# Routed experts: GpSimd loads the down matrices block by block with indirect transfers, SP loads gate and up alone

## The chip, the cores and the metric

One core of one Trainium2 chip runs the whole program. The time is the device time of one execution in microseconds (us). Engines are called PE (TensorE), DVE (VectorE), ACT (ScalarE), POOL (GpSimd) and SP (SyncE, which here only issues transfers).

## The reference

Two transformer blocks follow each other over 512 tokens of width 1024, in float32. The change touches only the last large stage, the routed experts of the second block. Cut to what matters:

```
scores = sigmoid(u @ w_router);  top_e = top 8 of 64 experts (within 4 of 8 groups)
xb  = u_pad[toks]                                   # tokens of one expert, gathered
hid = silu(xb @ we_gate[e]) * (xb @ we_up[e])       # 1024 -> 256
y   = (hid @ we_down[e]) * ws[:, None]              # 256 -> 1024
routed = segment_sum(y, token)                      # added back to the tokens
```

Each expert has three matrices of 1024 KB: gate, up and down.

## The kernel before

**Plan.** The tokens of an expert are cut into half blocks of 64 rows. DVE and PE work out a plan on the chip: the half blocks, sorted by expert, are dealt to four lanes, each lane taking a quarter of the list in order. One block holds 128 rows: block `b` with `p = b % 2` takes the next half block of lanes `2p` and `2p+1`. There are 48 blocks (24 pairs). Where a lane's next half block has the same expert as the one before it, the weights stay where they are; such a stretch is a run, and each run loads its expert once, into the lane's slot of `moe["gu"]` (gate and up) and of `moe["dn"]` (down). So each lane has one slot only, and a new matrix can be loaded once the last product that reads the slot is through.

**SP.** SP goes through the runs in order (`run(m)` reads expert, lane and the block that frees the slot, three register loads; `load` waits and issues). For each run it issues gate, then up, then down:

```
with sp.Fori(4, runs) as m:
    of = run(m)
    load(m, of, "we_gate", "gate_through", KD, ...)
    load(m, of, "we_up", "up_through", KD, ...)
    load_down(m, of)
```

Each `load` waits for two things: that the previous transfer of the same matrix kind has landed, and that the slot is free (`gate_through` is counted by ACT's SiLU, `up_through` and `down_through` by PE's last matmul). SP is one queue, so a wait for the down slot also holds the gate and up of the next run.

**PE.** For block `b`: the up phase (`block_up`, 64 matmuls, gate half then up half), the first four transposes of the next block's rows, two transposes of the hidden rows, the other four transposes, and the down phase (`block_down`, 16 matmuls). Both phases begin with `loads_needed(b)`, a register load of how many loads must have landed.

**ACT and DVE.** ACT copies the transposed rows (`block_rows`) and does the SiLU (`block_gate`). DVE multiplies by the up half (L2920), copies the transposed hidden rows (L2926) and scales the result into `moe["y"]` (L2934).

**POOL.** POOL serves the tokens: `gather` (L841, L844) fetches the 128 rows of a block from DRAM, three blocks ahead, `scatter` (L848, L854) adds the block's result back to DRAM, `weights` (L859) copies a column. Both are indirect transfers of 4 KB rows. A row whose index is out of bounds moves nothing. The order in POOL's queue is gather, scatter, weights, for each block; two scatters are never in flight together (`y_added`).

Of the kernel before, what the change touches and what calls it, by code (L numbers as in the profile page):

```python
# [7 lines left out]
P = 128  # L8
# [3 lines left out]
TT = T // P  # L12
# [13 lines left out]
E = 64  # L26
# [39 lines left out]
MAX_BLOCKS = MAX_HALVES // 2  # L66
PAD_ROW = 4 * T
# [3 lines left out]
def two_blocks(nc, A, out_T, u_rows, y_rows):  # L71
    f32 = mybir.dt.float32
    f32r = mybir.dt.float32r
    ALU = mybir.AluOpType
# [4 lines left out]
    with ctx:  # L79
# [109 lines left out]
        def rounded(name, shape, at):  # L189
# [63 lines left out]
                      for i, at in enumerate((split_at + 4 * (FT - 8) * T, arena_at + 4 * (ple["end"] + 12 * T)))]  # L253
# [21 lines left out]
                       shift=(2,)))  # L275
# [11 lines left out]
                                                      "own_key", "own_halves")] +  # L287
# [32 lines left out]

        rows_in = [ints(f"rows_in{i}", 1, u32) for i in range(2)]
# [281 lines left out]
        for v in range(STEPS):  # L603
# [7 lines left out]
            n = len(maps)  # L611
# [21 lines left out]
        def _(sp):  # L633
# [43 lines left out]
            def load_down(m, of):  # L677
                load(m, of, "we_down", "down_through", 2, moe["dn"])
# [12 lines left out]
            for m in range(2):  # L691
                of = run(m)
                load_up(m, of)
                load_down(m, of)
# [4 lines left out]
            load_down(2, of2)  # L699
            load_down(3, of3)  # L700
            with sp.Fori(4, runs) as m:
# [3 lines left out]
                load_down(m, of)  # L705
# [19 lines left out]
        def _(pool_eng):  # L725
# [114 lines left out]
            def gather(b, p):  # L840
                pool_eng.tensor_copy(rows_in[p][:, :], moe["idx"][:, bass.ds(b, 1)]).then_inc(S("rows_known"), 1)  # L841
                pool_eng.wait_ge(S("rows_known"), b + 1)
# [4 lines left out]
            def scatter(b, p, added):  # L847
# [7 lines left out]
                                            bounds_check=2 * Y_ROWS - 1, oob_is_err=False, compute_op=ALU.add).then_inc(S(f"y_added{p}"), 16)  # L855

# [19 lines left out]
            pool_eng.wait_ge(S("second_zeroed"), 16 * (TT - 2))  # L876
            scatter(0, 0, 1)
# [20 lines left out]
        def _(pe):  # L898
# [747 lines left out]

            def hidden_transposes(b, p):
# [5 lines left out]
            def block_down(b, p):  # L1653
                needed = loads_needed(b)
                for k in range(2):
                    pe.wait_ge(S("hT_done"), b * 2 + (k + 1))
                    if k == 0:
                        pe.wait_ge(S("we_down_in"), needed)
                    for half in range(2):
                        if k == 0:  # L1660
                            pe.wait_ge(S("y_copied"), b * 2 + (2 * TT + half - 1))
# [11 lines left out]
            def block(b, p, gathers):  # L1673
# [3 lines left out]
                hidden_transposes(b, p)  # L1677
                block_transposes(b + 1, 1 - p, gathers, 1)
# [4 lines left out]
            block(0, 0, 1)  # L1683
            with pe.Fori(1, pairs) as i:


                for b, p in ((i * 2 + (-1), 1), (i * 2, 0)):
                    block(b, p, i + 1)
# [1398 lines left out]
```

## Time and profile before

| | |
|---|---|
| median of 3 runs | 2215.12 us (2207.13 to 2215.75) |
| the profiled execution, its own time | 2209.77 us |
| its span in the profile | 2207.8 us |
| PE busy in the span | 97% |
| DVE, POOL, ACT busy | 55%, 34%, 32% |
| routed experts, first to last block | about 1585 to 2183 us |

The span runs from the first to the last instruction and is 2.0 us short of the execution's own time. In the routed experts (from about 1585 us) PE repeats one block after another, and 16 DMA engines carry weights, gathered rows and scattered rows side by side. A transfer issued by SP goes through queue q1, one issued by POOL through queue q0.

### The profile page before, as it was taken

The page shows a single profiled execution, that of the slowest core. Times are in us where ns is not written, and L with a number is a line of the kernel's source. Part 1 is how long each engine was busy: PE and PEld are TensorE (multiplying, and loading weights), DVE is VectorE, ACT ScalarE, POOL GpSimd, SP SyncE. Part 2 cuts the span into 40 slices and gives each one's busy share as a digit, 9 for nine tenths or more (in the row PEclk, how much of TensorE's full clock was granted, in tenths as well). Part 3 has the DMA queues.
Part 4 walks back from the last instruction along what each step waited for, and adds up shares of the span by engine and source line. Part 5 has one row for each costly group of instructions (what it writes and reads, how often), then busy time and mean ns, then how long its engine had stood idle before and what let it go on. Part 6 is the DMA issues. An engine that isn't in the chain of part 4 may idle for free.

```text
span 2207.8 us, 31566 instructions
## 1 busy us (share of the span) xinstructions
PE 2136.7 (97%) x11810; PEld 1536.7 (70%) x11811; DVE 1207.6 (55%) x1891; ACT 716.5 (32%) x1116; POOL 740.6 (34%) x462
## 2 busy tenths in 40 slices
PE   6999999999999999999999999999999999999898
PEld 5877567788878767777777778876565555555555
DVE  5566655889981448599999684246412112122113
ACT  5335664333342334344444345123111111111112
POOL 4331123434444324333333356441122222222222
PEclk9999899999999999999999999999999999999999
DMA  4220122454634212333333213322778899999885
GB/s 165 77 96 1 68 77 78 167 175 158 210 131 151 86 60 85 98 105 102 100 104 102 91 58 115 115 100 86 287 239 310 283 336 321 311 332 352 298 286 186
DMA packets 165535, 358.73 MB, mean 162 GB/s; under 512 B 12016, under 2 KB 101232, under 8 KB 146624
## 3 DMA queue, kind: packets, MB, share of 16 engines
q1 hardware_dynamic: 143360, 304.00, 38.3%
q0 software_dynamic: 15088, 38.69, 7.2%
q10 hardware_dynamic: 6992, 14.75, 2.0%
q8 instruction: 63, 1.03, 0.2%
q14 instruction: 32, 0.26, 0.0%
HBM read 340.87 MB, written 33.10 MB: 169 GB/s over the span
## 4 chain that ended last, share of the span: by engine, by line
PE 86%; DMA 5%; ACT 3%; DVE 2%; POOL 2%; issue 1%; SPq 0%; ACTq 0%; POOLq 0%; DVEq 0%
PE bank L911 25%; PE bank L1643 14%; PE bank L1334 12%; PE bank L1664 7%; PE bank L1233 4%; PE bank L1413 3%; DMA arena<-in_we_gate 2%; PE bank L1622 2%; PE bank L1047 1%; PE bank L1420 1%; DMA arena<-in_w_up 1%; PE bank L1498 1%; PE bank L920 1%; PE bank L921 1%; PE bank L1082 1%
## 5 line engine op out<-in xcount | busy, mean ns | idle before, releaser
L1643 PE MATMUL bank<-arena,hn 128*64 128x256 f32 x3072 | 346.7, 384 | 12.3 <-DMA arena<-in_we_gate 11.5
L1643 PEld LDWEIGHTS bank<-arena,hn 128*64 128x64 f32 x3072 | 232.8, 139 | 138.5 <-issue 43.9
L805 POOL TENSOR_TENSOR w_low_flat<-arena,in_high 128x1024 fp32r<-128x1024 f32 x71 | 184.3, 2617 | 278.4 <-ACT in_high L1968 278.3
L2920 DVE TENSOR_TENSOR inv<-inv,bank 128x128 f32<-128x128 f32 x96 | 23.3, 284 | 327.6 <-PE bank L1643 327.6
L1664 PE MATMUL bank<-arena 128*64 128x512 f32 x768 | 175.4, 598 | 5.1 <-DVE arena L2926 0.5
L772 POOL TENSOR_TENSOR w_low<-arena,w_high 128x2048 fp32r<-128x2048 f32 x22 | 103.7, 4712 | 160.1 <-ACT w_high L1890 160.1
L2934 DVE SCALAR_TENSOR_TENSOR sq<-bank,arena 128x512 f32<-128x512 f32 x96 | 72.1, 751 | 151.3 <-PE bank L1664 149.5
L1334 PE MATMUL bank<-in_x,in_high 128*128 128x512 f32 x384 | 154.2, 402 | 0.0
L1334 PE MATMUL bank<-in_x,w_low_flat 128*128 128x512 f32 x384 | 151.1, 393 | 0.0
L1334 PE MATMUL bank<-x_low,in_high 128*128 128x512 f32 x384 | 150.7, 392 | 0.0
L911 PE MATMUL bank<-x_high,w_high 128*128 128x512 f32 x336 | 133.4, 397 | 1.8 <-POOL w_low L772 1.8
L911 PE MATMUL bank<-x_high,w_low 128*128 128x512 f32 x336 | 132.4, 394 | 0.0
L911 PE MATMUL bank<-x_low,w_high 128*128 128x512 f32 x336 | 132.3, 394 | 0.0
L854 POOL DMA_INDIRECT y_halves<-sq,rows_out x47 | 75.5, 1606 | 155.0 <-DVE sq L2934 151.9
L2255 ACT ACTIVATE inv<-bank 128x256 f32<-128x256 f32 x48 | 18.4, 383 | 333.4 <-PE bank L1643 333.4
L1664 PEld LDWEIGHTS bank<-arena 128*64 128x64 f32 x768 | 52.6, 136 | 97.0 <-issue 96.7
L2250 ACT ACTIVATE hn<-bank 128x512 f32<-128x512 f32 x96 | 57.3, 597 | 185.8 <-PE bank L1622 185.8
L2479 DVE SCALAR_TENSOR_TENSOR arena<-arena,small 128x512 f32<-128x512 f32 x84 | 101.5, 1209 | 3.0
L841 POOL CAST rows_in<-arena 128x1 uint32 (+1 forms) x48 | 8.8, 183 | 262.0 <-PE bank L1622 249.2
L2367 DVE RECIPROCAL inv<-inv 128x512 f32<-128x512 f32 x20 | 67.0, 3352 | 53.9 <-ACT inv L1717 53.9
L744 POOL TENSOR_TENSOR w_low<-arena,z_w_high 128x2048 fp32r<-128x2048 f32 (+2 forms) x12 | 61.9, 5155 | 89.6 <-ACT z_w_high L1727 89.6
L1334 PEld LDWEIGHTS bank<-in_x,w_low_flat 128*128 128x128 f32 x384 | 72.1, 188 | 17.0
(499 smaller groups left out, 4887.2 us busy)
## 6 DMA issues: line engine op xcount, KB each, us to landing
arena<-in_we_gate SPq DMA_DIRECT2D x49, 1024.0 KB, 8.5
arena<-in_we_up SPq DMA_DIRECT2D x49, 1024.0 KB, 9.0
arena<-in_we_down SPq DMA_DIRECT2D x49, 1024.0 KB, 8.4
arena<-in_w_in SPq DMA_DIRECT2D x38, 1024.0 KB, 5.3
arena<-in_w_ada SPq DMA_DIRECT2D x12, 2048.0 KB, 7.8
arena<-in_w_up SPq DMA_DIRECT2D x22, 1024.0 KB, 10.6
arena<-in_w_in SPq DMA_DIRECT2D x17, 512.0 KB, 5.1
arena<-in_w_out SPq DMA_DIRECT2D x4, 2048.0 KB, 9.9
```

Of the source, the lines that this page charges most:

```text
L772: pool_eng.tensor_tensor(up_low(pair), w, up_high(pair).bitcast(f32), ALU.subtract)\
L805: pool_eng.tensor_tensor(in2_tile(j, "low"), in2_tile(j, "whole"), in2_tile(j, "high").bitcast(f32), ALU.subtract).then_inc(S("w_low"), 1)
L854: pool_eng.indirect_dma_start(y_rows, bass.IndirectOffsetOnAxis(rows_out[p][:, :], 0), moe["y"][:, p, :], None, bounds_check=2 * Y_ROWS - ...
L911: ins = nc.tensor.matmul(out, w, x, start=k == 0 and n == 0, stop=k == KD - 1 and n == 2)
L1233: ins = nc.tensor.matmul(banks[DOWN_BANK[t]][:, :], w, x, start=k == HID_ORDER[0] and n == 0, stop=k == HID_ORDER[-1] and n == 2)
L1334: ins = nc.tensor.matmul(banks[i % 2][:, :], w[:, k, :], x, start=k == 0 and n == 0, stop=k == KD - 1 and n == 2)
L1413: nc.tensor.matmul(banks[t][:, :], w[:, P * t:P * t + P], yn_high_tile(k), start=k == 0 and w is high, stop=False)
L1643: ins = nc.tensor.matmul(rows_of(banks[2 + part][:, 0:FE], c), columns_of(moe["xT"][:, p, :], k, c), moe["gu"][:, 2 * p + c, at:at + FE], ...
L1664: ins = nc.tensor.matmul(rows_of(banks[5 + half], c), columns_of(moe["hidT"][:, p, :], k, c), moe["dn"][:, 2 * p + c, at:at + 512], start= ...
L2367: nc.vector.reciprocal(inv[:, j % 2, :], inv[:, j % 2, :]).then_inc(S("qk_inv"), 1)
L2479: ins = nc.vector.scalar_tensor_tensor(out, w[:, k, :], C_ACT[:, k:k + 1], out, ALU.mult, ALU.add)
L2934: nc.vector.scalar_tensor_tensor(moe["y"][:, p, 512 * half:512 * half + 512], banks[5 + half][:, :], moe["wcol"][:, p:p + 1], moe["g2"][:, ...
```

## The change

SP issues gate and up only, except for the first down matrix of each of the four lanes (`first_down`). The other down matrices are loaded by POOL, once for each block: `load_down(b, p, known)` waits until block `b - 2` is through its down phase, copies two columns of row numbers, and issues two indirect transfers, one for each lane of the block. DVE works out the row numbers: in the first half block of a run, row `128 * expert + partition` of the down matrices seen as rows of 8 KB; in all others a number out of bounds, so that the transfer moves nothing. PE no longer reads how many down loads it needs; it waits for 32 per block on `down_loaded0` or `down_loaded1`, and does so (`down_free`) ahead of the second four transposes. PE's loop is shorter by one pair of blocks, which are written out.

```diff
-            def load_down(m, of):
-                load(m, of, "we_down", "down_through", 2, moe["dn"])
+            def first_down(m, of):
+                e, lane, free = of
+                if m > 0:
+                    sp.wait_ge(S("we_down_in"), m * 16)
+                sp.wait_ge(S("down_through"), free)
+                sp.nop(nofuse=True)
+                sp.dma_start(moe["dn"][:, m, :], A["we_down"][bass.ds(e, 1)].rearrange("a (p k) n -> p (a k n)", k=2))\
+                  .then_inc(S("we_down_in"), 16)
...
             with sp.Fori(4, runs) as m:
                 of = run(m)
                 load(m, of, "we_gate", "gate_through", KD, moe["gu"][:, :, 0:KD * FE])
                 load(m, of, "we_up", "up_through", KD, moe["gu"][:, :, KD * FE:2 * KD * FE])
-                load_down(m, of)
...
+            def load_down(b, p, known):
+                pool_eng.wait_ge(S("down_through"), b + 1)
+                pool_eng.tensor_copy(dn_now[p][:, :], dn_rows[:, bass.ds(b * 2, 2)]).then_inc(S("rows_known"), 1)
+                pool_eng.wait_ge(S("rows_known"), known)
+                for c in range(2):
+                    pool_eng.nop(nofuse=True)
+                    pool_eng.indirect_dma_start(moe["dn"][:, 2 * p + c, :], None, A["we_down"].rearrange("e (p k) n -> (e p) (k n)", k=2),
+                                                bass.IndirectOffsetOnAxis(dn_now[p][:, c:c + 1], 0), bounds_check=E * P - 1,
+                                                oob_is_err=False).then_inc(S(f"down_loaded{p}"), 16)
...
             with pool_eng.Fori(2, pairs) as i:
                 pool_eng.wait_ge(S("moe_tr"), i * 4 + (-2))
-                gather(i * 2, 0)
+                gather(i * 2, 0, i * 4 + (-2))
+                load_down(i * 2 + (-1), 1, i * 4 + (-1))
                 scatter(i * 2 + (-3), 1, i)
                 weights(i * 2 + (-1), 1)
                 pool_eng.wait_ge(S("moe_tr"), i * 4)
-                gather(i * 2 + 1, 1)
+                gather(i * 2 + 1, 1, i * 4)
+                load_down(i * 2, 0, i * 4 + 1)
                 scatter(i * 2 + (-2), 0, i)
                 weights(i * 2, 0)
+            load_down(pairs_but_one * 2 + 1, 1, pairs_but_one * 4 + 2)
...
+                if tt == 0:
+                    nc.tensor.matmul(banks[3][:, 2 * P:3 * P], pcol("dn_row").to_broadcast([P, P]), ident, start=True, stop=True)
...
+            def down_free(b, loaded, value):
+                pe.wait_ge(S(loaded), value)
+                for half in range(2):
+                    pe.wait_ge(S("y_copied"), b * 2 + (2 * TT + half - 1))
...
             def block_down(b, p):
-                needed = loads_needed(b)
                 for k in range(2):
                     pe.wait_ge(S("hT_done"), b * 2 + (k + 1))
-                    if k == 0:
-                        pe.wait_ge(S("we_down_in"), needed)
...
                 block_transposes(b + 1, 1 - p, gathers, 0)
                 hidden_transposes(b, p)
+                down_free(b, loaded, value)
                 block_transposes(b + 1, 1 - p, gathers, 1)
                 block_down(b, p)
...
+            step(nc.vector.tensor_scalar(pcol("dn_row"), pcol("new"), -float(NO_ROW), float(NO_ROW), ALU.mult, ALU.add))
+            counted_step(nc.vector.scalar_tensor_tensor(pcol("dn_row"), pcol("expert"), float(P), pcol("dn_row"), ALU.mult, ALU.add))
...
+            nc.vector.tensor_scalar(dn_rows, banks[3][:, 2 * P:3 * P], const("row"), None, ALU.add)
             nc.vector.tensor_copy(moe["ws"], banks[3][:, MAX_BLOCKS:2 * MAX_BLOCKS]).then_inc(S("blocks_known"), 1)
```

PE, in the loop over pairs, from the hidden transposes of a block to its down phase. Before:

```order
L1650 MATMUL bank<-shp,inv 128x128 [waits moe_hid] x2
L1622 MATMUL bank<-shp,hn 128x128 x4
L1632 TENSOR_LOAD shp
L1632 ISA x2
L1661 REGISTER_ALU [waits we_down_in,hT_done]
L1664 MATMUL bank<-arena 64x512 [waits y_copied]
```

The register load (L1632) stands between the transposes and the down phase. The same place in the changed kernel (there L1679 is the hidden transposes, L1646 the row transposes, L1688 the down phase):

```order
L1679 MATMUL bank<-shp,inv 128x128 [waits moe_hid] x2
L1674 REGISTER_ALU [waits down_loaded1]
L1674 REGISTER_ALU [waits y_copied]
L1646 MATMUL bank<-shp,hn 128x128 [waits y_copied]
L1646 MATMUL bank<-shp,hn 128x128 x3
L1688 MATMUL bank<-arena 64x512 [waits hT_done]
```

The register load is gone from between the transposes and the down phase, and the waits for the weights and for the result's banks now stand ahead of the second four transposes.

POOL, in its loop, one half of a turn. Before (L841 and L844 are the gather, L848 and L854 the scatter, L859 the weights):

```order
L841 COPY rows_in<-arena 128x1
L842 REGISTER_ALU
L844 DMA hn<-u_rows,rows_in 128x1024 [waits rows_known]
L848 ISA
L848 COPY rows_out<-arena 128x1
L849 REGISTER_ALU
L850 ISA [waits rows_back]
L852 REGISTER_ALU [waits y_copied]
L854 DMA y_halves<-sq,rows_out 1024x1024 [waits y_added0]
```

Between the gather and the scatter stand a copy and its wait only. The same place in the changed kernel (L852 is the gather, L867 to L871 the down loads, L862 the scatter):

```order
L852 DMA hn<-u_rows,rows_in 128x1024 [waits rows_known]
L867 ISA [waits down_through]
L867 COPY arena<-arena 128x2
L868 REGISTER_ALU
L871 DMA arena<-in_we_down,arena 128x2048 [waits rows_known]
L871 DMA arena<-in_we_down,arena 128x2048
L856 ISA
L856 COPY rows_out<-arena 128x1
L857 REGISTER_ALU
L858 ISA [waits rows_back]
L860 REGISTER_ALU [waits y_copied]
L862 DMA y_halves<-sq,rows_out 1024x1024 [waits y_added0]
```

A copy and two indirect transfers, behind a wait for PE's down phase, now stand between the gather and the scatter.

## Rows read from the trace of the kernel before

**Rows 1.** The page, its first line.

```profile
span 2207.8 us, 31566 instructions
```

**Rows 2.** The stretches view of the expert stage: busy us of each engine, clock, DMA.

```profile
1590.00:2160.00 570.00, 553.88 (x4124) 321.40 (x4122) 113.62 (x276) 72.56 (x138) 146.26 (x226) 0.99 0.87 301
```

**Rows 3.** Waits of PE, 1580 to 2150 us: total us, times, longest.

```profile
PE bank L1643 <- DMA arena<-in_we_gate: 11.5, 2, 6.5
```

**Rows 4.** The chain that ended last, around its two stops: start, us, what.

```profile
1765.03 3.67 PE bank L1664 x16
...
1771.84 7.47 DMA arena<-in_we_gate
...
1788.39 9.41 DMA arena<-in_we_gate
1797.93 8.71 PE bank L1643 x64
...
1808.15 3.65 PE bank L1664 x16
...
2061.81 3.67 PE bank L1664 x16
...
2096.13 9.78 PE bank L1643 x64
...
2107.46 3.65 PE bank L1664 x16
```

**Rows 5.** The timeline of one undisturbed block: start, us, engine, line, operation.

```profile
1619.17 0.60 PE L1622 MATMUL bank<-shp,hn 128*128 128x128 f32 x4
1619.18 0.49 DVE L2926 COPY arena<-bank 128x128 f32<-128x128 f32 x2 [0.23 <-PE bank L1650]
1619.86 3.65 PE L1664 MATMUL bank<-arena 128*64 128x512 f32 x16
...
1620.94 1.07 POOL L844 DMA_INDIRECT hn<-u_rows,rows_in  x1 [0.81 <-POOL rows_in L841]
...
1623.34 7.08 PE L1643 MATMUL bank<-arena,hn 128*64 128x256 f32 x64
...
1625.18 1.60 POOL L854 DMA_INDIRECT y_halves<-sq,rows_out  x1 [2.97 <-DVE sq L2934]
...
1632.03 0.18 POOL L841 CAST rows_in<-arena 128x1 uint32 x1 [5.05 <-PE bank L1622]
```

**Rows 6.** The timeline at the first stop.

```profile
1760.73 0.35 SPq L670 DMA_DIRECT2D arena<-in_we_gate  x1
...
1763.73 0.34 SPq L670 DMA_DIRECT2D arena<-in_we_up  x1
...
1768.91 0.34 SPq L670 DMA_DIRECT2D arena<-in_we_down  x1
...
1772.17 0.38 ACT L2255 ACTIVATE inv<-bank 128x256 f32<-128x256 f32 x1 [6.60 <-PE bank L1643]
...
1789.20 3.65 PE L1664 MATMUL bank<-arena 128*64 128x512 f32 x16
```

**Rows 7.** Waits of SP, 1580 to 2200 us.

```profile
SPq L669 <- PE bank L1664: 96.9, 21, 4.7
```

**Rows 8.** DMA queues, 1765 to 1800 us: packets, MB, share of 16 engines.

```profile
q1 hardware_dynamic: 1605, 11.70, 84.7%
q0 software_dynamic: 738, 1.58, 15.3%
```

**Rows 9.** The timeline ahead of the stage: the last tables of the plan.

```profile
1561.57 3.73 PE L1577 MATMUL bank<-arena 128*128 128x128 f32 x32
...
1563.55 1.22 DVE L2897 TENSOR_TENSOR arena<-arena,shp 128x1024 f32<-128x1024 f32 x1 [3.10 <-PE bank L1577]
...
1574.49 0.28 DVE L2908 TENSOR_SCALAR arena<-bank,shp 128x64 f32<-128x64 f32 x1
```

**Rows 10.** The page, DMA issues of the down matrices: count, KB each, us to landing.

```profile
arena<-in_we_down SPq DMA_DIRECT2D x49, 1024.0 KB, 8.4
```

More of the change, by code:

```diff
@@ L66 @@
 MAX_BLOCKS = MAX_HALVES // 2
+NO_ROW = 1 << 20
 PAD_ROW = 4 * T
@@ L274, in two_blocks @@
                        hidT=(2, 2 * P), wcol=(2,), idx=(MAX_BLOCKS,), ws=(MAX_BLOCKS,), out=(MAX_BLOCKS,),
-                       shift=(2,)))
+                       shift=(2,), dnr=(P,), dnn=(2, 2)))
         moe["X"] = hn[:, 0:4, :].rearrange("p (a b) n -> p a (b n)", a=2)
@@ L319, in two_blocks @@
         block_i = ints("block_i", TT * TOP, i32)
+        dn_rows = moe["dnr"].bitcast(u32)
+        dn_now = [moe["dnn"][:, i, :].bitcast(u32) for i in range(2)]
         rows_in = [ints(f"rows_in{i}", 1, u32) for i in range(2)]
@@ L693, in _ @@
                 load_up(m, of)
-                load_down(m, of)
+                first_down(m, of)
             of2, of3 = run(2), run(3)
@@ L698, in _ @@
             load_up(3, of3)
-            load_down(2, of2)
-            load_down(3, of3)
+            first_down(2, of2)
+            first_down(3, of3)
             with sp.Fori(4, runs) as m:
@@ L704, in _ @@
                 load(m, of, "we_up", "up_through", KD, moe["gu"][:, :, KD * FE:2 * KD * FE])
-                load_down(m, of)
             for p in range(2):
@@ L838, in _, with gather @@
                                        ALU.mult).then_inc(S("sh_hid"), 1)
-            def gather(b, p):
+            def gather(b, p, known=None):
                 pool_eng.tensor_copy(rows_in[p][:, :], moe["idx"][:, bass.ds(b, 1)]).then_inc(S("rows_known"), 1)
-                pool_eng.wait_ge(S("rows_known"), b + 1)
+                pool_eng.wait_ge(S("rows_known"), b + 1 if known is None else known)
                 pool_eng.nop(nofuse=True)
@@ L876, in _ @@
             pool_eng.wait_ge(S("second_zeroed"), 16 * (TT - 2))
+            load_down(2, 0, 5)
             scatter(0, 0, 1)
@@ L1672, in _, with block @@
             pairs = pairs_but_one + 1
-            def block(b, p, gathers):
+            def block(b, p, gathers, loaded, value):
                 block_up(b, p)
@@ L1682, in _ @@
                 block_transposes(0, 0, 1, half)
[L1683 to L1688, printed above, removed]
+            block(0, 0, 1, "we_down_in", 32)
+            block(1, 1, 2, "we_down_in", 64)
+            with pe.Fori(1, pairs_but_one) as i:
+                for p in range(2):
+                    block(i * 2 + p, p, i + (p + 1), f"down_loaded{p}", i * 32)
+            block(pairs_but_one * 2, 0, pairs, "down_loaded0", pairs_but_one * 32)
             block_up(pairs_but_one * 2 + 1, 1)
             hidden_transposes(pairs_but_one * 2 + 1, 1)
+            down_free(pairs_but_one * 2 + 1, "down_loaded1", pairs_but_one * 32)
             block_down(pairs_but_one * 2 + 1, 1)
```

5 lines of the change are left out of this document (2 added, 3 removed).

## The prediction

> **What bounds the kernel now.** The page's first line gives the span to set the sum against [rows 1]. The stretches view of the expert stage shows who is full: PE is busy 553.9 of 570 us at a granted clock of 0.99, while the DMA engines are busy 0.87 of the time [rows 2]. So the stage is bound by PE, with the DMA engines close behind. The list of waits says how little PE waits: 11.5 us in two pieces, both for a gate matrix [rows 3]. The chain that ended last gives the full price of the two stops. From the down phase at 1808.15 to the one at 2061.81 lie 21 blocks, so one block takes 253.66 / 21 = 12.08 us. From 1765.03 to 1808.15 there are three blocks, which should take 36.2 us and take 43.1: 6.9 us lost. From 2061.81 to 2107.46 again three blocks, 45.6 us: 9.4 us lost. That is 16.3 us, more than the wait of 11.5, because the up phase behind each stop takes 8.7 and 9.8 us where an undisturbed one takes 7.1 [rows 4, 5]. What the change can win on transfers is at most these 16.3 us. Anything else must come out of the 12.08 us of a block.
>
> **Part 1: SP no longer waits for the down slot.** SP waited 96.9 us in 21 pieces for PE's down phase [rows 7]; the question is which of these waits reaches PE. At the first stop it does. The gate and up of a lane go out at 1760.73 and 1763.73. Then SP stands until the down phase ends at 1768.7, issues down at 1768.91, and 2.93 us later (register loads) the gate of the next lane [rows 4, 6]. From there the chain is three landings of gate matrices one behind the other, the last of 9.4 us, and PE goes on at 1797.93, when it wanted to at 1789.20 + 3.65 = 1792.85 [rows 4, 6].
>
> In the changed kernel SP issues the second gate 2.93 us after the up at 1763.73, at about 1766.7, 5.2 us sooner. If that one lands within 6 us, the third gate goes out when its slot is free, behind the SiLU that ends at 1772.55 [rows 6], at about 1772.8, and the fourth when the third has landed. PE wants the fourth at 1792.85, so two landings have 20.0 us: the stop is gone if a landing takes 10.0 us or less.
>
> How long is a landing then? In the burst q1 moves 11.70 MB in 0.847 of 35 us, which is 2.66 us of all engines for one matrix of 1.05 MB, and q0 takes 5.4 us for the gathers and scatters of three blocks, 1.8 us a block [rows 8]. Three matrices in flight behind each other today make 3 x 2.66 / 0.847 = 9.4 us, which is what the chain shows (7.5 and 9.4) [rows 4]. After the change q1 holds only two matrices, 5.3 us if q0 is idle. But q0 then carries two down matrices a block on top, 2 x 2.66 + 1.8 = 7.1 us of work. If two busy queues share evenly, that takes 14.2 us, more than a block, so in a burst q0 always has work, and a landing takes 2 x 2 x 2.66 = 10.6 us. Two of them miss the 20.0 us by 1.2. Between the ends 5.3 and 10.6 I stand near the upper one, since both queues are full there. I leave 2.5 us at each stop for what remains, the slower clock behind a stop included, and book **11 us** of the 16.3. The bounds are 16.3 (both stops gone) and nothing. The bytes don't change: a matrix is loaded once for each run, as before, and a row out of bounds costs next to none of the engines' time, as with the padding rows of the gathers that are in the 1.8 us.
>
> **A rule that speaks against it.** The row above shows q1 taking 84.7% while q0 has little to do, and says nothing of two full queues. The Trainium skill, "DMA: Bandwidth & Descriptors", section "SWDGE vs HWDGE vs iDMA", states that the software and hardware paths feed different queues inside each DMA engine, between which the engine takes turns. By that rule the landing is the 10.6 us end, and of the 11 us the stops give back still all but 1.2 us each before the clock's share. The same page, section "Rules for kernel authors", says that spreading transfers over issuing engines gives no bandwidth and only saves issue time; that would put all of the gain into the 5.2 us of SP's earlier issue. It makes of the two stops 10.4 us instead of 11.
>
> **Part 2: PE between the transposes and the down phase.** In an undisturbed block the second four transposes start at 1619.17 and end at 1619.77, and the down phase starts at 1619.86 [rows 5]. A following group can begin before its forerunner's end: the up phase starts at 1623.34, 0.17 us before the down phase's end at 1623.51. So the down phase could start at 1619.60. Its operand isn't what is late: DVE's first copy of two ends at 1619.43 [rows 5]. The 0.26 us belong to what PE's queue holds there: a register load, its two followers and the waits for weights and banks, all behind the transposes. The register load goes, and the waits move ahead of the second transposes, where they may cost some of it again. So the gain is between 0 and 0.26 us; in 47 blocks 0 to 12. I take 0.15, as three waits with register arithmetic remain: **7 us**. The waits themselves are long satisfied outside bursts (the banks since DVE's scaling of the block before). In a burst a late down matrix would now also hold four transposes, 0.6 us, which ACT needs before the next up phase; it has 3.65 us of down phase as cover.
>
> **Part 3: POOL.** New in each block are a copy, a wait for it, and two indirect transfers. The wait is 0.81 us, a gather costs 1.07 and a scatter 1.60 [rows 5]. The trace has no indirect transfer of 8 KB rows. The nearest is the gather, same direction and as many rows, so 0.2 + 0.8 + 2 x 1.07 = 3.1 us; with the dearer 1.60, 4.2 us; if the price goes by bytes on top of that, 3.2 us each and 7.4. POOL is idle for 5.05 us ahead of the next gather, and the new work can start some 0.9 us before today's scatter could, since it waits for PE's end and not for DVE's scaling [rows 5]. So there are 6.0 us of room, and at 3.1 or 4.2 the cost is **0**. Queued behind the new work is the scatter, 2 to 3 us later; the result buffer it must empty is wanted two blocks on, and at 12.08 us a block that is covered. The gather behind it is three blocks ahead of use. The down matrix itself is issued about 2 us after the down phase of block b - 2 and wanted some 20 us later: with the 14.2 us above it is in time.
>
> **Part 4: the start.** DVE has an added operation of 128 columns ahead of the copy on which the first gather waits; the like one of 64 columns takes 0.28 us [rows 9]. PE has one more matmul in front of 32 that take 3.73 us, 0.12 us each [rows 9]. Together **0.5 us** more. DVE's two one-column operations lie before the tables, where DVE waits 3.10 us for PE later on [rows 9]. Without that cover they would cost about as much as that operation, 0.3 us each.
>
> **The sum:** 2207.8 - 11 - 7 + 0.5 = 2190.3 us of span, 2192.3 with the 2.0 outside it. The profiled execution (2209.8) stands 5.3 us under the median of the runs (2215.1), which themselves lie 8.6 apart. 17.5 us off the one is 2192.3 and off the other 2197.6; I write 2197.
>
> **Rivals.**
> - **Only one of the two gains comes.** The stops are merely moved, since the DMA engines are at full share either way, or the wait ahead of the transposes costs what the register load did. For it: DMA is busy 0.87 on average [rows 2]. Against it: the first stop's chain begins with SP's wait. It leaves 5 to 10 us, 2205 to 2210: not to be told from no change, since about 0.5% (11 us) is what a measurement of this kernel can tell.
> - **The evenly shared queues make new stops.** The down matrices of q0 are wanted 8 us later than the gates of the same block, yet get half of the engines. Wherever three or four lanes change together, a gate lands after 10.6 us or more (12.4 if a block's whole q0 work goes first), 2 x 12.4 - 20 = 4.8 us at each of the two stops and perhaps as much at four more stretches: 29 us lost instead of 16.3, less the 7 of part 2: 2221. It decides from a landing of 11.5 us. By the skill's rule of taking turns, named above, the stop would be 1.2 us and this rival would not come.
> - **POOL becomes the bound.** If an indirect transfer of 8 KB rows costs POOL 3.2 us, each block needs 7.4 - 6.0 = 1.4 us more than it has, 64 us in 46 blocks, less the 24 us that the gathers are ahead: 40 slower, 2248 with part 2. It decides from 2.5 us each. Against it: the gather's 1.07.
> - **The change doesn't do what it says**, and the out-of-bounds rows are moved or are dear: 96 down matrices instead of 49 [rows 10] would be 47 x 2.66 = 125 us of DMA in a stage that has 74 free: some 50 us slower. The gathers' padding speaks against it.
>
> **How the numbers follow.** Forecast 0.52, one gain only 0.28, new stops 0.10, POOL 0.07, rows not skipped 0.03. The likeliest's own range is 2184 to 2206. The range 2183 to 2224 takes in the second and third case and leaves out POOL, the skipped rows and some of both sides. Faster by over 0.5%: 0.52; within: 0.29; slower: 0.19.
>
> **What would show it.** Right: no SP wait for the down phase; at both places where today the chain shows gate matrices, PE waits under 3 us; the down phase 0.1 to 0.25 us nearer to the transposes; two POOL transfers of 1.1 to 1.6 us before each scatter; a block of about 11.9 us. Wrong: waits of PE for gate or down matrices elsewhere, a gather that PE waits for, POOL transfers of over 2.5 us, or a block of 12.1 us.

## The result

The changed kernel took 2200.23 us (median of 6 runs, 2195.37 to 2204.64), the kernel before 2214.38 us on the same chip (6 runs, 2205.67 to 2216.81). The ratio is 0.9948, with a 95% interval of 0.993 to 0.9966: faster by about 11.5 us, by just over 0.5%. The ratio takes in all runs; the two medians alone lie 14.2 us apart. Run again in a later session it gave 0.9949 (0.9931 to 0.9968). The prediction was 2197 us.

The page of the changed kernel, its first line, comes first, then the stretches view of the expert stage (us; busy us of PE, weight load, DVE, ACT, POOL; granted clock; share of the DMA engines; GB/s).

```profile
span 2202.8 us, 31560 instructions
```

```profile
1590.00:2160.00 570.00, 564.49 (x4192) 319.47 (x4190) 113.81 (x276) 73.00 (x139) 248.27 (x367) 0.99 0.87 304
```

Against [rows 1, 2]: the span is 5.0 us shorter, less than the 11.5, since the profiled execution of the changed kernel was its slowest (2204.64 us) and that of the kernel before lay under its median (2209.77 against 2214.38). PE is busy 10.6 us more of the same 570 us, at the same clock, and the DMA engines are as busy as before. POOL has 102 us more to do, and none of PE's waits below is for POOL's own work.

The waits of PE (us in total, times, longest), 1585 to 2155 us, then those of SP, 1580 to 2200 us:

```profile
PE bank L1667 <- DMA arena<-in_we_gate: 5.5, 2, 2.9
PE bank L1646 <- DMA hn<-u_rows,rows_in: 3.9, 1, 3.9
```

```profile
SPq L672 <- DMA arena<-in_we_up: 67.9, 16, 5.4
SPq L672 <- PE bank L1667: 61.6, 25, 2.5
SPq L672 <- DMA arena<-in_we_gate: 58.6, 31, 4.8
```

PE waits for a gate in the same two places, 5.5 us where it was 11.5 [rows 3], and nowhere in the blocks for a down matrix. The 3.9 us for gathered rows lie ahead of the first block, at the first gather of all (PE goes on at 1586.26); the kernel before waits there too, 2.65 us, until 1582.41. SP's wait for the down phase (96.9 us [rows 7]) is gone from the loop. SP now waits most for its own transfers.

**Where the time went.** The stage, from the first down phase to the 48th, can be read from two timeline rows of each kernel (start, us, engine, line, operation). Before:

```profile
1595.69 1.90 PE L1664 MATMUL bank<-arena 128*64 128x512 f32 x7
...
2179.88 3.65 PE L1664 MATMUL bank<-arena 128*64 128x512 f32 x16 [0.51 <-DVE arena L2926]
```

After:

```profile
1599.47 1.94 PE L1688 MATMUL bank<-arena 128*64 128x512 f32 x8
...
2174.16 3.65 PE L1688 MATMUL bank<-arena 128*64 128x512 f32 x16 [0.28 <-DVE arena L2957]
```

That is 584.19 us before and 574.69 after, 9.5 less. I split it with the 48 starts: the mean of the periods that hold no stop is the block, and what the 47 periods hold above 47 blocks is what the stops cost. A period counts as holding a stop from 0.3 us above the median of all periods on; where many periods are a little long (down_late, extra_two, no_skip) the split is rough. The same sum for every kernel, from one profile each:

| kernel | stage | block | stops in all |
|---|---|---|---|
| before | 584.2 | 12.08 | 16.2 |
| changed | 574.7 | 12.03 | 9.2 |
| changed, second run | 573.7 | 12.03 | 8.1 |
| one_load | 577.6 | 11.91 | 17.8 |
| waits_ahead | 583.4 | 11.98 | 20.3 |
| waits_behind | 569.9 | 11.92 | 9.8 |
| waits_behind_2 | 569.7 | 11.92 | 9.6 |
| short_loads | 570.8 | 11.91 | 10.8 |
| down_late | 589.6 | 12.08 | 22.0 |
| extra_two | 587.5 | 12.20 | 14.2 |
| sp_still_waits | 592.2 | 12.03 | 27.0 |
| no_skip | 630.5 | 12.08 | 63.0 |

So of the 9.5 us, 7.0 come from the stops (16.2 - 9.2) and 2.4 from the block (0.052 x 47). The second run of the changed kernel differs by 1.1 us in its stops, which says how far a stop total of one profile can be trusted. Ahead of the stage the profiled execution was 3.8 us late, behind it 0.7, which leaves the 5.0 of the span. Most of the 3.8 isn't the change's. DVE's first operation of the plan, ahead of every operation that the change adds, already starts 2.37 us later. Before, it and the first gather's issue, and the same two after:

```profile
1513.41 0.14 DVE L2747 TENSOR_SCALAR arena<-shp 128x1 f32<-128x1 f32 x1
...
1577.16 1.10 POOL L844 DMA_INDIRECT hn<-u_rows,rows_in  x1 [0.93 <-POOL rows_in L841]
```

```profile
1515.78 0.14 DVE L2775 TENSOR_SCALAR arena<-shp 128x1 f32<-128x1 f32 x1
...
1580.00 1.11 POOL L852 DMA_INDIRECT hn<-u_rows,rows_in  x1 [0.93 <-POOL rows_in L849]
```

From the one to the other lie 63.75 us before and 64.22 after: the change costs 0.47 us there. The other 0.94 us lie between the first gather's issue and the first down phase (18.53 us before, 19.47 after). Of these, 0.54 is the first up phase, 9.45 us before and 9.99 after, at mean granted clocks of 0.75 and 0.70. In the second run of the changed kernel the same up phase took 7.13 us at a granted clock of 1.00, so this isn't the change's either. In waits_behind, whose program up to the stage is the same, the first down phase starts at 1594.93, earlier than before. The offset goes with the execution.

**The first stop.** SP's timeline in the changed kernel has the first gate's issue:

```profile
1763.61 0.34 SPq L673 DMA_DIRECT2D arena<-in_we_gate  x1
```

and the chain that ended last goes on from the up (start, us, what):

```profile
1766.62 0.34 SPq L673
...
1767.35 1.23 SPq L661
...
1770.53 8.64 DMA arena<-in_we_gate
...
1779.42 9.62 DMA arena<-in_we_gate
...
1789.29 9.08 DMA arena<-in_we_gate
...
1798.51 8.81 PE bank L1667 x64
```

The second gate goes out 3.9 us after the up of its forerunner, with no wait between, so the cause of [rows 4, 6] is gone. But it is still a chain of three landings, not two: the first takes 8.64 us, so that the third gate, too, waits for a landing and not for its slot, and the fourth's issue is set by landings alone. The stops cost 9.2 us though PE waits only 5.5. The rest is the up phase behind each: at this stop PE stood 2.87 us, then the granted clock was 0.54 from 1798.5 to 1801.5, nearly the lower of its two levels (1.2 of 2.4 GHz), and the up phase took 8.81 us where the one at 1759.49 took 6.93. The queues in the burst, 1765 to 1800 us (packets, MB, share of the 16 engines):

```profile
q1 hardware_dynamic: 1064, 7.80, 54.0%
q0 software_dynamic: 1136, 5.59, 46.7%
```

q0 has gone from 15.3% to 46.7%, q1 from 84.7% to 54.0% [rows 8]: two busy queues share nearly evenly here. The Trainium skill, "DMA: Bandwidth & Descriptors", section "SWDGE vs HWDGE vs iDMA", says that each DMA engine takes turns between the software and the hardware queue. The trace agrees with that; the page gives no shares.

**One block.** The timeline of an undisturbed one:

```profile
1621.87 0.66 PE L1646 MATMUL bank<-shp,hn 128*128 128x128 f32 x4
1622.06 0.48 DVE L2951 TENSOR_TENSOR inv<-inv,bank 128x128 f32<-128x128 f32 x2 [6.22 <-PE bank L1667]
...
1622.40 0.53 PE L1679 MATMUL bank<-shp,inv 128*128 128x128 f32 x2
...
1622.88 0.65 PE L1646 MATMUL bank<-shp,hn 128*128 128x128 f32 x4
1623.46 3.65 PE L1688 MATMUL bank<-arena 128*64 128x512 f32 x16
...
1623.70 0.18 POOL L849 CAST rows_in<-arena 128x1 uint32 x1 [2.01 <-PE bank L1646]
1624.71 1.05 POOL L852 DMA_INDIRECT hn<-u_rows,rows_in  x1 [0.83 <-POOL rows_in L849]
...
1627.31 0.19 POOL L867 COPY arena<-arena 128x2 uint32 x1 [1.54 <-PE bank L1688]
1628.38 1.03 POOL L871 DMA_INDIRECT arena<-in_we_down,arena  x1 [0.88 <-POOL arena L867]
1629.71 1.00 POOL L871 DMA_INDIRECT arena<-in_we_down,arena  x1 [0.30 <-issue]
```

The down phase starts 0.58 us after the second transposes, where it was 0.69 [rows 5]. An indirect transfer that brings 8 KB rows costs POOL 1.0 us, no more than a gather of 4 KB rows. The new work runs from 1627.31 to 1630.71, 3.4 us. POOL keeps 2.0 us of idle time before the next gather, where it had 5.05, and 1.5 before the copy: 3.5 us of room are left.

### The profile page after: what moved, and what is told of

Read it like the earlier page. It is cut to its first block, busy times and chain, and to the rows that moved or that the text cites. A ratio compares the mean times of both kernels' runs of the same rounds, so it can differ in the third digit from the quotient of the medians.

```text
span 2202.8 us, 31560 instructions
## 1 busy us (share of the span) xinstructions
PE 2139.4 (97%) x11812; PEld 1526.5 (69%) x11813; DVE 1214.1 (55%) x1894; ACT 716.2 (33%) x1116; POOL 839.5 (38%) x600
## 3 DMA queue, kind: packets, MB, share of 16 engines
q8 instruction: 64, 1.05, 0.2%
## 4 chain that ended last, share of the span: by engine, by line
PE 85%; DMA 5%; DVE 3%; ACT 2%; POOL 2%; issue 1%; SPq 1%; ACTq 0%; POOLq 0%; DVEq 0%
PE bank L933 25%; PE bank L1667 14%; PE bank L1356 12%; PE bank L1688 7%; PE bank L1255 4%; PE bank L1435 3%; DMA arena<-in_we_gate 2%; PE bank L1646 2%; PE bank L1069 1%; PE bank L1442 1%; DMA arena<-in_w_up 1%; PE bank L1520 1%; PE bank L942 1%; PE bank L1104 1%; PE bank L950 1%
## 5 line engine op out<-in xcount | busy, mean ns | idle before, releaser
L1667 PEld LDWEIGHTS bank<-arena,hn 128*64 128x64 f32 x3072 | 225.5, 139 | 139.0 <-issue 35.4
L1688 PE MATMUL bank<-arena 128*64 128x512 f32 x768 | 175.4, 598 | 0.3 <-DVE arena L2957 0.3
L862 POOL DMA_INDIRECT y_halves<-sq,rows_out x47 | 76.2, 1620 | 110.4 <-DMA y_halves<-sq,rows_out 64.7
L871 POOL DMA_INDIRECT arena<-in_we_down,arena x92 | 92.9, 1010 | 56.2 <-POOL arena L867 39.7
L1688 PEld LDWEIGHTS bank<-arena 128*64 128x64 f32 x768 | 51.1, 136 | 90.4 <-issue 83.0
```

The costliest lines, as they stand in the source:

```text
L862: pool_eng.indirect_dma_start(y_rows, bass.IndirectOffsetOnAxis(rows_out[p][:, :], 0), moe["y"][:, p, :], None, bounds_check=2 * Y_ROWS - ...
L871: pool_eng.indirect_dma_start(moe["dn"][:, 2 * p + c, :], None, A["we_down"].rearrange("e (p k) n -> (e p) (k n)", k=2), bass.IndirectOffs ...
L1667: ins = nc.tensor.matmul(rows_of(banks[2 + part][:, 0:FE], c), columns_of(moe["xT"][:, p, :], k, c), moe["gu"][:, 2 * p + c, at:at + FE], ...
L1688: ins = nc.tensor.matmul(rows_of(banks[5 + half], c), columns_of(moe["hidT"][:, p, :], k, c), moe["dn"][:, 2 * p + c, at:at + 512], start= ...
```

## The experiments

The theory after the result: the stops shrank because SP no longer stands behind the down phase, and what is left of them comes from landings on evenly shared queues; the block got shorter because PE's second register load went, and lost two thirds of that again (0.115 of 0.17 us) to the waits ahead of the transposes. The rivals: the stops shrank through the other queue or the slots alone, whatever SP does; the block got shorter through the moved waits; POOL, or down matrices that come late, already take something. Ratios are against the kernel before, measured on the same chip in the same session.

### one_load: the kernel before, with one register load in PE

```diff
-            def block_down(b, p):
-                needed = loads_needed(b)
+            def block_down(b, p, needed):
...
-                block_up(b, p)
+                needed = block_up(b, p)
...
-                block_down(b, p)
+                block_down(b, p, needed)
```

> The kernel before, with one edit on PE: the down phase uses the count of loads that the up phase of the same block has read, so the register load between the second transposes and the down phase is gone; SP still loads all three matrices, POOL is untouched. Theory (the register load is late at the down phase): the block falls from 12.08 us to 11.90 (11.83 to 12.00), the two stops stay at 6.9 and 9.4 us, the whole is 5 to 11 us faster. Rival (the waits behind the transposes are what is late, or nothing is): the block stays at 12.05 to 12.08, the whole within 2 us of before.

Measured: 2202.98 us, ratio 0.9957 (0.9938 to 0.9976). The block is 11.91 us, 0.17 less, 8 us over the stage; the stops are 17.8 us in all. So this edit alone, without any change to the transfers, gives in the block more than the whole change did there (2.4 us), and nothing in the stops. A third stop, of 1.6 us, has appeared; one profile doesn't say whether the faster blocks made it.

### waits_behind and waits_behind_2: the changed kernel, waits behind the transposes

```diff
-                down_free(b, loaded, value)
                 block_transposes(b + 1, 1 - p, gathers, 1)
+                down_free(b, loaded, value)
```

> The changed kernel with PE's waits for the down matrices and for the result's banks put back behind the second transposes. Theory (in the changed kernel these waits ahead of the transposes cost back a part of what the register load gave): the block falls from 12.04 us to 11.85 to 11.98, 3 to 8 us less in all than the changed kernel (its median was 2200), stops as in the changed kernel (4.8 and 4.6). Rival (waits cost the same in either place, or more next to the down phase): 12.03 to 12.10 a block, within 2 us of the changed kernel or slower.

> The changed kernel with PE's waits behind the second four transposes, once more, for a tighter interval beside the other. If the shorter block is real, the ratio is 0.993 again, with a block of 11.92 us; if the first run was luck it lies at 0.995, as the changed kernel.

Measured: 2195.51 us, 0.993 (0.991 to 0.9951), and again on another chip 2193.82 us, 0.9938 (0.9916 to 0.996). The block is 11.92 us in both, 0.115 shorter than the change's 12.03, 5.4 us over the stage. The timeline shows where. In this kernel:

```profile
1629.78 0.53 PE L1679 MATMUL bank<-shp,inv 128*128 128x128 f32 x2
1630.14 0.60 PE L1646 MATMUL bank<-shp,hn 128*128 128x128 f32 x4
1630.67 3.65 PE L1688 MATMUL bank<-arena 128*64 128x512 f32 x16
```

From the transposes of the hidden values to the second four transposes are 0.36 us, and from there to the down phase 0.53: 0.89. In the changed kernel's block above they are 0.48 and 0.58: 1.06. In its next block they are 0.38 and 0.58, 0.96:

```profile
1634.48 0.53 PE L1679 MATMUL bank<-shp,inv 128*128 128x128 f32 x2
1634.86 0.65 PE L1646 MATMUL bank<-shp,hn 128*128 128x128 f32 x4
1635.44 1.08 PE L1688 MATMUL bank<-arena 128*64 128x512 f32 x4
```

These two alternate through the loop, as blocks of 12.08 and 11.98 us, and the differences of the sums from 0.89 (0.17 and 0.07) are, within 0.01, those of the blocks from 11.92. PE waits for none of the three semaphores there; the time goes all the same, on both sides of the transposes.

It isn't the place of the waits alone. In the changed kernel blocks 0 and 1 are written out ahead of the loop, and their waits, in the same place, are for constants. Block 1 there:

```profile
1610.49 0.53 PE L1679 MATMUL bank<-shp,inv 128*128 128x128 f32 x2
1610.85 0.60 PE L1646 MATMUL bank<-shp,hn 128*128 128x128 f32 x4
1611.38 3.65 PE L1688 MATMUL bank<-arena 128*64 128x512 f32 x16
```

That is 0.36 and 0.53, as in waits_behind, and the period that ends there is 11.91 us; it is 11.91 or 11.92 in after_again, down_late, sp_still_waits and no_skip too, whose PE program is the same. So a satisfied wait for a constant costs nothing that shows. What costs comes with the blocks in the loop, where the values that are waited for are worked out in registers. That it is this arithmetic is likely, but no run changes it alone.

### waits_ahead: the kernel before, one register load, the waits moved ahead

```diff
 (one_load, and)
+            def down_free(b, needed):
+                pe.wait_ge(S("we_down_in"), needed)
+                for half in range(2):
+                    pe.wait_ge(S("y_copied"), b * 2 + (2 * TT + half - 1))
...
+                down_free(b, needed)
                 block_transposes(b + 1, 1 - p, gathers, 1)
-                block_down(b, p, needed)
+                block_down(b, p)
```

> The kernel before with one register load (as in the experiment that left only the second load out, block 11.91 us), and PE's waits for the down matrix and the two banks moved ahead of the second four transposes, as the change has them; nothing of the change on SP or POOL. If those waits, placed there, cost what the runs with and without them put on them (12.03 - 11.92), the block is 12.03 us, 5.4 us more over the stage than with the register load alone, and the ratio is 0.998. If the 0.115 us comes from something else of the change (its two semaphores, POOL's transfers), the block stays at 11.91 and the ratio at 0.996.

Measured: 2209.23 us, 0.999 (0.9974 to 1.0006). Neither number of the two expectations: the block is 11.98 us. The waits in that place cost 0.07 us here, some 60% of the 0.115. The block is as long as the shorter of the two blocks of the changed kernel, and its block 0, the only one with constants for the banks, again shows 0.36 and 0.53 us. The other 0.05 is the 0.1 us that every second block of the changed kernel takes more, and comes with something else of the change; its waits for down matrices, on one of two semaphores against the loop's counter, are the candidate, but no run takes that apart. The stops are 20.3 us against 17.8 in one_load; one execution of each doesn't say whether the waits did that.

### sp_still_waits: the changed kernel, SP still behind the down phase

```diff
                 load(m, of, "we_up", "up_through", KD, moe["gu"][:, :, KD * FE:2 * KD * FE])
+                sp.wait_ge(S("down_through"), of[2])
+                sp.nop(nofuse=True)
```

> The changed kernel, in which SP after each run's up matrix waits until the down slot is free, as it did before, but issues nothing then. Theory (the smaller stops of the changed kernel come from SP no longer standing in that wait): the stops grow from 4.7 and 4.5 us to 6.5 to 10 each and there may be a third; the block stays at 12.03 us; 4 to 12 us slower than the changed kernel. Rival (the stops are smaller because the down matrices no longer stand in q1's line between the gates, whatever SP waits for): stops of 4 to 5.5 us, within 2 us of the changed kernel.

Measured: 2220.8 us, 1.004 (1.0027 to 1.0053), slower than before. SP's and PE's waits:

```profile
SPq L715 <- PE bank L1690: 112.0, 25, 4.7
```

```profile
PE bank L1669 <- DMA arena<-in_we_gate: 13.5, 7, 6.1
PE bank L1669 <- DMA arena<-in_we_up: 5.6, 6, 1.6
```

The block is that of the changed kernel, the stops are 27.0 us instead of 9.2, nine instead of two. With the down matrices on POOL's queue and SP's wait kept, the gates go out about as late as before and land later, while q0 takes 48.5% of the engines. At the first stop 10.6 us lie between the first gate's issue and the second's (11.1 before, 6.9 in the changed kernel), and the three landings take 9.6, 9.2 and 9.8 us (7.5, 8.6 and 9.4 before). All of the gain in the stops thus comes from SP's earlier issue, and with SP held back the shared queues cost 11 us (27.0 - 16.2). This is the rival of new stops as it looks when SP doesn't get ahead.

### down_late: the changed kernel, POOL's loads behind the scatter

```diff
-                load_down(i * 2 + (-1), 1, i * 4 + (-1))
                 scatter(i * 2 + (-3), 1, i)
                 weights(i * 2 + (-1), 1)
+                load_down(i * 2 + (-1), 1, i * 4 + (-1))
```

> The changed kernel with POOL's order scatter, weights, down loads instead of down loads, scatter, weights; the down matrices reach queue q0 some 3 us later in each block. Theory (in a burst the two queues share the engines evenly, and the down matrices of q0 hold up the gates of q1): the gates land sooner and each stop falls from 4.7 us to 2 to 3.5, 2 to 5 us less in all; the scatter waits less for the one before. Rival A (the stop is set by the bytes of a burst or by SP's own chain): stops of 4.5 to 5. Rival B (the down matrices are now late): PE waits for them, slower than the changed kernel.

Measured: 2211.21 us, 1.0005 (0.9987 to 1.0023): all of the gain is gone. PE's waits:

```profile
PE bank L1646 <- DMA arena<-in_we_down,arena: 13.0, 6, 3.0
```

and the chain, at a stop of 4.3 us:

```profile
1782.90 0.76 DVE sq L2965
...
1784.59 0.09 POOL y_halves L862
...
1787.40 1.05 POOL arena L871
1788.75 19.60 DMA arena<-in_we_down,arena
1808.57 1.11 PE bank L1646 x4
```

No gate stops PE any more. Now the down matrices do: their issue stands behind the scatter, which waits for DVE's scaling, and the landing takes 19.6 us. My estimate of it was 14.2. This is rival B of the expectation. As the change orders them they are in time; some 3 us later they are the bound.

### extra_two: the changed kernel, two more indirect transfers a block

They bring nothing anywhere: all of their rows are out of bounds, and the result is the same.

```diff
                                                 oob_is_err=False).then_inc(S(f"down_loaded{p}"), 16)
+                for c in range(2):
+                    pool_eng.nop(nofuse=True)
+                    pool_eng.indirect_dma_start(nowhere[:, 2 * p + c, :], None, ...,
+                                                bass.IndirectOffsetOnAxis(no_rows[:, c:c + 1], 0), bounds_check=E * P - 1,
+                                                oob_is_err=False).then_inc(S(f"down_loaded{p}"), 16)
...
(the waits for down_loaded: i * 64 instead of i * 32)
```

> The changed kernel with two more indirect transfers on POOL in each block, all of whose rows are out of bounds, so that they move nothing; this adds 2 x 1.3 us to POOL's chain of a block, where the changed kernel leaves it 2.0 us idle. Theory (POOL has slack of its own and is some two blocks ahead): 0.6 us a block too much, 28 us over the stage, eaten by the lead of about 24 us: 0 to 6 us slower than the changed kernel. Rival (POOL's chain reaches PE at once): 0.6 x 46 = 28 us slower or more.

Measured: 2215.82 us, 1.0015 (0.9996 to 1.0033). That is some 16 us slower than the changed kernel, between the 0 to 6 of the theory and the 28 of the rival: neither was right. The groups of POOL from 1590 to 2160 us (line, engine, operation, names, count | busy us, mean ns of one | idle before):

```profile
L874 POOL DMA_INDIRECT arena<-in_we_down,arena x88 | 88.7, 1008 | 52.4 <-POOL arena L870 38.5 <-issue 13.9
L879 POOL DMA_INDIRECT nowhere<-in_we_down,no_rows x88 | 88.3, 1004 | 26.8 <-issue 26.8
```

A transfer that moves nothing costs POOL as much as one that moves 1 MB in 8 KB rows, 1.00 us, and 0.30 between two: 2.6 us more a block, of 3.5 that were left. From the timeline of one block:

```profile
1727.07 1.63 POOL L865 DMA_INDIRECT y_halves<-sq,rows_out  x1 [1.04 <-PE bank L1656]
...
1737.39 0.66 PE L1656 MATMUL bank<-shp,hn 128*128 128x128 f32 x4
1737.87 0.49 DVE L2961 TENSOR_TENSOR inv<-inv,bank 128x128 f32<-128x128 f32 x2 [6.52 <-PE bank L1677]
...
1738.15 1.63 POOL L865 DMA_INDIRECT y_halves<-sq,rows_out  x1 [1.04 <-issue]
```

Behind a long wait for a scatter, POOL works through a block in 11.08 us without a gap, from scatter to scatter, still under PE's 12.0. It isn't the bound even now, it only catches up slowly. What makes the block 12.20 us is DVE: its first product starts 0.48 us after the transposes in this block and 0.3 to 0.4 in most, 0.19 in the changed kernel (1621.87 and 1622.06 above), and PE waits for it. DVE's own rows are no longer than before (284 ns against 283), and what holds it back I didn't trace. So the causal step from POOL's extra work to DVE's delay is not shown. With 8 us of blocks (0.17 x 47), 5.0 of stops and 4.3 ahead of the stage, the span is 17.7 us longer than the changed kernel's. So POOL's own time isn't what costs here, but more work on POOL isn't free either.

### no_skip: the changed kernel, down matrices loaded for every block

```diff
-step(... pcol("dn_row"), pcol("new"), -float(NO_ROW), float(NO_ROW), ...)
+step(... pcol("dn_row"), pcol("new"), 0.0, 0.0, ...)
```

The same matrices are loaded again in each block; the result is the same.

> The changed kernel with the row numbers in bounds in every half block, so that each down matrix is loaded again for every half block (96 loads instead of 49). It prices the skipping. Theory: 47 x 2.66 = 125 us more work for the DMA engines, of which 70 to 75 us were free: 40 to 70 us slower than the changed kernel, with PE waiting for gate and down matrices through the whole stage. Rival (a skipped row costs nearly as much as a moved one): within 10 us of the changed kernel.

Measured: 2259.65 us, 1.0216 (1.0196 to 1.0236), 48.6 us slower than before. The stretches view of the stage:

```profile
1590.00:2190.00 600.00, 559.50 (x4030) 309.41 (x4030) 108.92 (x268) 70.70 (x135) 236.88 (x350) 0.96 0.96 354
```

The DMA engines are at 0.96 now, the granted clock of PE is down to 0.96 as well, and the stops take 63 us. The transfers on POOL, all with rows now, cost it 1013 ns each, against 1010 where half of them are skipped. The rival of rows that aren't skipped was priced at some 50 us. Not skipping costs 59 us against the changed kernel, 48.6 against the kernel before, so the price was about right, and the change isn't it.

### short_loads: waits_behind, SP's register loads without their range checks

```diff
 (waits_behind, and for the expert and the lane, but not for the count of free slots)
-                        sp.value_load(plan[...], min_val=0, max_val=3),
+                        nc.values_load(plan[...], engines=[SP], ..., skip_runtime_bounds_check_because=...)
```

> The changed kernel with PE's waits behind the second transposes (median 2195.5) and with two of SP's three register loads of each run without the run-time check of their range, which takes some 0.6 us off SP's way from an up to the next gate. Theory (SP's register loads stand in the chain of gates that ends in a stop): each stop is 0.3 to 0.8 us shorter, 1 us in all, not to be told from that kernel by time. Rival (the chain is set by the landings alone): stops of 4.8 to 5.0 as there.

Measured: 2194.41 us, 0.9927 (0.9908 to 0.9946), beside 0.993 for waits_behind alone. The first stop is 6.7 us, the second 4.2, where waits_behind has 4.9 and 5.0. That isn't a gain that can be told. Nor does the run decide the question: at the first stop the way from SP's up to its next gate became only 0.2 us shorter (3.67 us, 3.85 in waits_behind), not the 0.6 expected, while the three landings differ by up to 1.0 us (9.5, 9.3 and 9.2 against 8.5, 9.6 and 9.0).

### after_again: the changed kernel once more

> The changed kernel itself once more, as the measure for the others of this call and for what differs from run to run: a block of 12.03 us, stops of 4 to 5.5 us; where the stage begins (1588.1 us in its first profile, 1584.8 in that of the kernel before) the two earlier stages decide, and if the change itself cost 3.3 us there it begins at 1587 or later again. By the theory that the change costs 0.5 us ahead of the first block, the time from the start of the shared expert's last matmuls to the first block is within 1.5 us of before.

Measured: 2199.34 us, 0.9949 (0.9931 to 0.9968); block 12.03 us, stops 4.0 and 4.0. The blocks alternate again, but the first odd block of the loop also takes 12.08 us, so the extra 0.1 us isn't tied to the place in the code. The stage begins at 1590.0 us, later still than the 1588.1 of the first profile. Of that the change has 0.47 us again: from the plan's first large reduce on DVE to the first gather's issue are 35.93 us, 35.46 in the kernel before.

## Why the prediction was right, and where its numbers were off

- **Time and sign:** 2197 forecast, 2200.2 measured; faster by 11.5 us where 17.5 were booked. The mechanism was the forecast one in both parts, but the sizes were not: in the stage 18 us were booked and 9.5 and 10.5 came in the two profiles, a little over half. That the time lies only 3 us off is in part luck, since the executions of one kernel spread over 9 us.
- **Part 1, the stops:** 11 us booked, 7.0 measured (8.2 in the second run). The step that failed is "If that one lands within 6 us, the third gate goes out when its slot is free". The second gate took 8.64 us, with q0 at 45% of the engines from 1770 to 1780 us. So there were three landings of 8.6, 9.6 and 9.1 us where two in 20.0 us had been counted. Each was under the upper end of 10.6 that I had taken, but three of them leave a stop of 4.7 us. The second stop, 4.5 us, has the same chain (8.9, 9.2 and 9.1 us). From the first gate's issue to the second's are 6.9 us (1763.61 to 1770.53), where it was 11.1 (1760.73 [rows 6] to 1771.84 [rows 4]). That is 4.2 us sooner, not 5.2: one of SP's register loads took 1.23 us on the chain, which makes 3.9 us from the up where 2.93 had been read. sp_still_waits shows that the sooner issue is the whole cause of the gain: without it the stops are 27.0 us. The prediction's sum by the rule of taking turns doesn't come out either: two stops that keep 1.2 us each give back 13.9 us of 16.3, not less than 11; what was booked left 2.5 us at each stop, and 4.7 and 4.5 stayed.
- **Part 2, PE:** 0.15 us a block booked, 0.052 measured. The size of the register load was right in kind (0.17 by one_load, inside the 0 to 0.26). What failed is the share given to "the waits move ahead of the second transposes, where they may cost some of it again": they cost 0.115, of which waits_ahead shows 0.07 without anything else of the change. The written-out blocks, with constants in these waits, lose nothing, so the place alone isn't the cost; the values in the loop's registers are the likely one.
- **Part 3, POOL:** right. 1.01 and 1.00 us with 0.3 between were measured for what had been bounded by 1.07 and 1.60; the cost was 0. The room of 6.0 us was about right: 3.4 used and 3.5 left. That extra_two is slower all the same, with DVE late in most blocks, is a price that my sum of POOL's own time didn't have. Booked too lightly was the landing of the down matrices, "with the 14.2 us above it is in time". It was in time, but in a burst of down_late it takes 19.6 us, and that run shows how near the edge it is.
- **Part 4, the start:** 0.5 booked, 0.47 measured. The two one-column operations cost nothing, as forecast, but the cover was another than the 3.10 us: DVE waits for PE right behind the place where they were put in, 1.26 us before and 0.65 after.
- **The rivals:** new stops did not come, except where SP was held back. Only one gain: both came, each smaller. POOL is not the bound, and the rows are skipped; no_skip, 59 us slower than the changed kernel, is near the price worked out for them.

What stays open is the 0.1 us that every second block of the changed kernel takes more, whether register arithmetic is what makes the waits cost, what holds DVE back in extra_two, and why the gate landed 8.6 us behind its issue rather than 10.6. The best version is waits_behind (0.993 and 0.9938). It beats the kernel before clearly. Against the changed kernel (0.9948 and 0.9949) the block's 5.4 us show in the traces, while the intervals of the ratios overlap. It has the transfers of the change and the full gain of the dropped register load.

## What to carry to other kernels

Take a change apart by what each queue loses, and test the smallest part by itself: here a register load between two short groups of matmuls was worth 8 us in the kernel before, about as much as the new transfers gave in the stops (7.0). Moving a load to another queue lets the first queue's loads go out sooner but doesn't make DMA time: here the two queues then shared nearly evenly, and the early issue had to outweigh the longer landings. A wait that is satisfied can still cost time in PE's queue between short instructions, here where its value was worked out in the loop; put it behind what doesn't need it, and measure.

## What the runs showed of the hardware

- An indirect transfer of 128 rows costs POOL 1.00 us if all rows are skipped, 1.01 with rows of 8 KB, 1.05 with gathered rows of 4 KB, 1.62 as an adding scatter, and 0.30 lies between two in a row: for loads the price goes by the transfer and not by bytes.
- Two busy queues, one of software descriptors and one of hardware descriptors, got 46.7% and 54.0% of the engines in the burst of the changed kernel, and a matrix of 1 MB on the latter took 8.6 to 9.6 us to land. On the former the slower of two landed after 19.6 us in down_late.
- A register load with its checks in PE's queue, between four transposes and a group of 16 matmuls, was visible as 0.17 us a block. Three waits that PE didn't stand in, moved from behind those transposes to ahead of them, cost 0.07 us (waits_ahead) where their values were worked out in the loop, and nothing in the written-out blocks that wait for constants (0.36 and 0.53 us around the transposes either way).
- Behind a stop of 2.87 us PE's mean granted clock was 0.54 over the next 3.0 us, and the up phase of 64 matmuls took 8.81 us where it took 6.93 at a granted clock of 1.00.
